# Weight tiles of a two-layer transformer kernel, moved to other byte positions in SBUF

## Chip, cores and metric

The kernel runs on one core of one Trainium2 chip. The metric is the device time of one execution in microseconds. Before the change the median of two runs is 2096.75 us (2096.28 to 2097.22).

## What is computed

Two transformer layers over 512 tokens (16 meta tokens are put ahead of the first) with a width of 1024, batch 1, all in float32. Cut to the projections, which are nearly all of the work:

```python
# first layer
p = rms_norm(h) @ w_in                       # pooling, attention, convolution, gates
y_a, y_b, y_c = pool(p) @ w_a, sparse_attention(p) @ w_b, conv(p) @ w_c
h = h + (g0 * y_a + g1 * y_b + g2 * y_c) @ w_o
h = h + (silu(gate) * up) @ w_down           # gate, up = rms_norm(h) @ w_gate_up, d_ff 2816
x = rms_norm(h)[16:]
# second layer
x = x + 0.5 * swiglu(rms_norm(x))            # d_ff 2816
x = x + merged(forgetting_attention, stick_breaking_attention) @ w_out
x = x + 0.5 * swiglu(rms_norm(x))            # d_ff 2816
x = x + sigmoid(rms_norm(x) @ w_ple_gate) * (p @ w_ple_proj)
```

## The kernel before

Activations lie transposed: feature on the partition, token on the free axis. hT (1024 x 528) is the residual. For a projection, each normed activation is split into a high and a low part, xh and xl, of 8 tiles with 128 x 576 columns, of which 528 are used (16 meta columns, then 512 tokens).

Weights come in 174 chunks. A chunk holds 2048 columns of 128 partitions: 8 contraction tiles of 256 output features. SyncE loads chunk c into raw[:, c % 2]. ScalarE copies it to whi as float32r (`high`, L1005; in the two attention stages of the second layer piece by piece, L1305), GpSimd subtracts to get wlo (`low`, L454, four instructions per chunk), and TensorE reads both. So raw, whi and wlo have two slots each, and a chunk's slot is c % 2. The next high tile of a slot is written when the chunk that used it is done.

TensorE makes three matmuls per contraction tile (`passes`, L543 to L547). The weights are the loaded operand and the activation is streamed:

```python
pe.matmul(o, w_of(whi), xhi, start=first, stop=False)    # L545
pe.matmul(o, w_of(whi), xlo, start=False, stop=False)    # L546
return pe.matmul(o, w_of(wlo), xhi, start=False, stop=last)   # L547
```

with `w_of = lambda wt: wt[:, s, w * k + o0:w * k + o0 + m]`. For a full chunk the piece of contraction tile k begins 1024 k bytes into the slot, plus 512 for the second half of the outputs; both are multiples of 256. The streamed piece is `hi[:, k, META:TM]`: 512 columns, 64 bytes into a row of 2304 bytes. Six chunks of the first layer (C_U to C_CB - 1) and the latent chunk C_LAT stream all 528 columns, in two parts of 264 (1056 bytes).

Where the streamed operand is not xh and xl it is: fh and fl in the three down projections (`ffn`, 528 matmuls each, three chunks of 8, 8 and 6 contraction tiles), ath, mh, m2h, ah, coh, yfh and ysh and their low parts in the mixer projections, pTh in the last. In `tokens` (L832 to L834, four chunks: the values of the two attentions of the second layer) xh and xl are loaded and whi and wlo are streamed, 256 columns at a time. C_FL is a chunk of 8 tiles with eight output features, 32 bytes each. `norm_sums` (L596 to L601), `head_sums` (L805) and the transposes (L759, L896, L903) are plain float32 matmuls with ones, onesblk or ident.

The order of the work is written out by hand, engine by engine; in the attention stages the single steps of the attention are set between the contraction tiles of chunks.

The tiles are allocated one behind the other in SBUF, in the order of the listing. By the built program, these are the first bytes in a partition, and that modulo 256:

```
tile        before          after
xh          18496  (64)     18496  (64)
xl          36928  (64)     36928  (64)
raw         55424  (128)    55424  (128)
whi slot 0  71808  (128)    71808  (128)
whi slot 1  80000  (128)    80128  (0)
wlo slot 0  88192  (128)    88512  (192)
wlo slot 1  96384  (128)    96832  (64)
rs          104576 (128)    105152 (192)
ident       113024 (128)    113600 (192)
arena, fh0  118144 (128)    118656 (128)
fh1         118272 (0)      118784 (0)
fh2         118336 (64)     118848 (64)
```

fh0 serves the first layer's FFN, fh1 and fh2 the two of the second layer; the low parts fl lie at the same place modulo 256. The operands of the mixer projections and pTh lie in the arena at 128 modulo 256.

Of the kernel before, what the change touches and what calls it, by code (L numbers as in the profile page):

```python
# [21 lines left out]
F32R = mybir.dt.float32r  # L22
# [4 lines left out]
P = 128  # L27
# [8 lines left out]
CH = 2048  # L36
# [67 lines left out]
def build(nc, I, out):  # L104
    with ExitStack() as ctx:
        def sb(name, shape, dt=F32):
            return ctx.enter_context(nc.sbuf_tensor(name, shape, dt))
# [9 lines left out]
        eps = sb("eps", [P, 1])  # L117
        m8 = sb("m8", [P, 8])
        raw = sb("raw", [P, 2, CH])
        whi = sb("whi", [P, 2, CH], F32R)  # L120
        wlo = sb("wlo", [P, 2, CH], F32R)
        rs = sb("rs", [P, TM])
        rt = sb("rt", [P, TM])
        sq = sb("sq", [P, TM])
# [16 lines left out]
        rtok = sb("rtok", [P, QB])  # L141
        fbias = sb("fbias", [8, 1])
        arena_cols = 27648
        pad = sb("pad", [P, (128 - (nc.sbuf_base + 31) // 32 * 32) % 256 // 4 or 64])
        start = (nc.sbuf_base + 31) // 32 * 32
        arena = sb("arena", [P, arena_cols])

# [1877 lines left out]
```

## Time and profile before

| | |
|---|---|
| runs, median | 2096.75 us |
| profiled execution, its own time | 2097.18 us |
| its span, first to last instruction | 2095.4 us |
| mean granted TensorE clock | 0.999 |
| TensorE matmul / weight load busy | 2053.9 / 1671.5 us |
| VectorE / ScalarE / GpSimd busy | 884.6 / 754.2 / 999.5 us |
| DMA | 184 MB, mean 88 GB/s |

The profiled execution is 0.4 us over the median. A matmul's recorded duration includes its way through the array and overlaps with the next matmul; its end is modelled. So the sum of durations is more than the time, and the pace of TensorE is the distance between two starts.

### The profile page before, as it was taken

The page shows a single profiled execution, that of the slowest core. Times are in us where ns is not written, and L with a number is a line of the kernel's source. Part 1 is how long each engine was busy: PE and PEld are TensorE (multiplying, and loading weights), DVE is VectorE, ACT ScalarE, POOL GpSimd, SP SyncE. Part 2 cuts the span into 40 slices and gives each one's busy share as a digit, 9 for nine tenths or more (in the row PEclk, how much of TensorE's full clock was granted, in tenths as well). Part 3 has the DMA queues.
Part 4 walks back from the last instruction along what each step waited for, and adds up shares of the span by engine and source line. Part 5 has one row for each costly group of instructions (what it writes and reads, how often), then busy time and mean ns, then how long its engine had stood idle before and what let it go on. Part 6 is the DMA issues. An engine that isn't in the chain of part 4 may idle for free.

```text
span 2095.4 us, 26593 instructions
## 1 busy us (share of the span) xinstructions
PE 2053.9 (98%) x9561; PEld 1671.5 (80%) x9561; DVE 884.6 (42%) x1394; ACT 754.2 (36%) x1038; POOL 999.5 (48%) x753
## 2 busy tenths in 40 slices
PE   8999999999999999999999999998899999999999
PEld 7798886688888888888888887886578888888877
DVE  6788735534333321343333124565653533331114
ACT  6412224434222223322222234666654332222232
POOL 5345442145555554455554445554434455554443
PEclk9999999999999999999999999999999999999999
DMA  4232331113333323333332232111113333332232
GB/s 156 71 96 81 101 100 61 41 60 100 101 100 100 92 88 107 95 96 88 97 100 91 95 96 81 61 50 52 41 61 101 100 99 88 94 100 95 91 105 81
DMA packets 250057, 184.01 MB, mean 88 GB/s; under 512 B 7040, under 2 KB 247168, under 8 KB 249984
## 3 DMA queue, kind: packets, MB, share of 16 engines
q1 hardware_dynamic: 249296, 182.74, 29.0%
q8 instruction: 44, 0.72, 0.1%
q10 hardware_dynamic: 688, 0.31, 0.1%
q14 instruction: 29, 0.24, 0.0%
HBM read 180.93 MB, written 2.10 MB: 87 GB/s over the span
## 4 chain that ended last, share of the span: by engine, by line
PE 89%; DVE 4%; ACT 2%; POOL 2%; issue 1%; DMA 0%; SPq 0%; DVEq 0%; ACTq 0%; POOLq 0%
PE ps L545 27%; PE ps L547 27%; PE ps L546 27%; POOL wlo L454 2%; DVE sc L1435 1%; PE ps L766 1%; PE ps L751 1%; PE ps L832 1%; PE ps L834 1%; PE ps L833 1%; DVE pu L1936 1%; PE ps L909 1%; DVE ssum L1563 0%; PE ps L765 0%; ACT whi L1305 0%
## 5 line engine op out<-in xcount | busy, mean ns | idle before, releaser
L454 POOL TENSOR_TENSOR wlo<-raw,whi 128x512 fp32r<-128x512 f32 (+1 forms) x692 | 938.2, 1386 | 978.3 <-ACT whi L1005 924.7
L545 PE MATMUL ps<-xh,whi 128*128 128x512 f32 (+2 forms) x1912 | 736.6, 385 | 12.9 <-DVE xl L1435 7.4
L547 PE MATMUL ps<-xh,wlo 128*128 128x512 f32 (+2 forms) x1912 | 723.2, 378 | 0.0
L546 PE MATMUL ps<-xl,whi 128*128 128x512 f32 (+2 forms) x1912 | 722.8, 378 | 0.0
L1005 ACT ACTIVATE whi<-raw 128x2048 fp32r<-128x2048 f32 (+1 forms) x159 | 297.5, 1871 | 802.3 <-PE ps L547 799.8
L545 PEld LDWEIGHTS ps<-xh,whi 128*128 128x128 f32 (+1 forms) x1912 | 359.4, 188 | 82.9 <-issue 11.7
L547 PEld LDWEIGHTS ps<-xh,wlo 128*128 128x128 f32 (+1 forms) x1912 | 358.6, 188 | 68.4
L546 PEld LDWEIGHTS ps<-xl,whi 128*128 128x128 f32 (+1 forms) x1912 | 359.4, 188 | 64.5 <-issue 2.5
L1489 DVE TENSOR_TENSOR tmp<-ps,rs 128x512 f32<-128x512 f32 x148 | 102.1, 692 | 325.8 <-PE ps L547 308.6
L545 PE MATMUL ps<-fh,whi 128*128 128x512 f32 x528 | 207.3, 393 | 0.0
L546 PE MATMUL ps<-fl,whi 128*128 128x512 f32 x528 | 207.3, 393 | 0.0
L547 PE MATMUL ps<-fh,wlo 128*128 128x512 f32 x528 | 207.3, 393 | 0.0
L1435 DVE SCALAR_TENSOR_TENSOR hT<-ps,hT 128x512 f32 x40 | 27.6, 691 | 279.0 <-PE ps L547 278.9
L1514 DVE TENSOR_TENSOR tmp<-tmp 128x512 f32<-128x512 f32 x66 | 90.2, 1367 | 114.3 <-ACT tmp L1047 114.2
L547 PEld LDWEIGHTS ps<-fh,wlo 128*128 128x128 f32 x528 | 99.0, 187 | 23.2
L546 PEld LDWEIGHTS ps<-fl,whi 128*128 128x128 f32 x528 | 99.0, 187 | 23.0
L545 PEld LDWEIGHTS ps<-fh,whi 128*128 128x128 f32 x528 | 99.0, 187 | 23.0
L1010 ACT ACTIVATE xh<-hT,vec (+1 forms) x48 | 34.5, 725 | 127.2 <-DVE hT L1435 127.2
L1049 ACT ACTIVATE fh<-tmp 128x512 f32 x66 | 41.8, 633 | 101.2 <-DVE tmp L1514 101.2
L1517 DVE TENSOR_TENSOR fl<-tmp,fh 128x512 f32 x66 | 51.1, 774 | 61.2 <-ACT fh L1049 61.2
L1435 DVE SCALAR_TENSOR_TENSOR xl<-hT,vec,xh (+1 forms) x48 | 46.0, 968 | 55.1 <-ACT xh L1010 54.9
L1047 ACT ACTIVATE tmp<-tmp 128x512 f32<-128x512 f32 x66 | 40.4, 612 | 2.9 <-DVE tmp L1489 2.9
(296 smaller groups left out, 2178.3 us busy)
## 6 DMA issues: line engine op xcount, KB each, us to landing
raw<-in_w_in SPq DMA_DIRECT2D x90, 512.0 KB, 4.6
raw<-in_w_gate_up SPq DMA_DIRECT2D x44, 512.0 KB, 4.7
raw<-in_ffn_w_gate SPq DMA_DIRECT2D x44, 512.0 KB, 4.0
raw<-in_ffn_w_up SPq DMA_DIRECT2D x44, 512.0 KB, 5.2
raw<-in_ffn_w_down SPq DMA_DIRECT2D x32, 512.0 KB, 4.3
raw<-in_w_down SPq DMA_DIRECT2D x16, 512.0 KB, 4.0
raw<-in_ffn_w_down SPq DMA_DIRECT2D x16, 384.0 KB, 3.4
raw<-in_w_b SPq DMA_DIRECT2D x8, 512.0 KB, 4.1
```

The lines of the kernel that those rows point to most:

```text
L454: ins = pool.tensor_tensor(wlo[:, c % 2, cs], raw[:, c % 2, cs], whi[:, c % 2, cs].bitcast(F32), ALU.subtract)
L545: pe.matmul(o, w_of(whi), xhi, start=first, stop=False)
L546: pe.matmul(o, w_of(whi), xlo, start=False, stop=False)
L547: return pe.matmul(o, w_of(wlo), xhi, start=False, stop=last)
L1005: act.activation(whi[:, c % 2, 0:n], raw[:, c % 2, 0:n], ACT.Copy).then_inc(w_hi, 1)
L1010: act.activation(one(xh, nn)[:, lo:TM], one(hT, nn)[:, lo:TM], ACT.Copy, scale=col(vec, lin(gain + n, per, i))).then_inc(xh_done, 1)
L1047: act.activation(tmp[:, 1, :], tmp[:, 0, :], ACT.Silu).then_inc(silu_done, 1)
L1049: act.activation(one(fh[f], lin(n, per, i)), tmp[:, 3, :], ACT.Copy).then_inc(h_hi, 1)
L1435: return dve.scalar_tensor_tensor(o, a, s, b, op0, op1)
L1489: dve.tensor_tensor(o, ps[0:o.shape[0], bank(c, t), :], rsx[0:o.shape[0]], ALU.mult).then_inc(acc_free, 1)
L1514: dve.tensor_tensor(tmp[:, 3, :], tmp[:, 1, :], tmp[:, 2, :], ALU.mult).then_inc(h_done, 1)
L1517: dve.tensor_tensor(one(fl[f], nn), tmp[:, 3, :], one(fh[f], nn).bitcast(F32), ALU.subtract).then_inc(h_split, 1)
```

## The change

High and low weight tiles get rows of 2080 columns, of which 2048 are used as before; between them stands a tile of 16 columns that nothing uses. So the four places (high or low, slot 0 or 1) differ modulo 256 bytes. The pad ahead of the arena is left out where its size would be zero, and the arena begins at 128 modulo 256 as before. The instructions of all five engines stand in the same order, with the same operands in the same sizes; only addresses differ. Of the tiles between wlo and the arena (rs, rt, sq, ssum, ident, identr, ones, causalr, strictr, onesblk and small ones) all move by 64 modulo 256.

```diff
-        whi = sb("whi", [P, 2, CH], F32R)
-        wlo = sb("wlo", [P, 2, CH], F32R)
+        whi = sb("whi", [P, 2, CH + 32], F32R)
+        aside = sb("aside", [P, 16])
+        wlo = sb("wlo", [P, 2, CH + 32], F32R)
...
-        pad = sb("pad", [P, (128 - (nc.sbuf_base + 31) // 32 * 32) % 256 // 4 or 64])
+        lead = (128 - (nc.sbuf_base + 31) // 32 * 32) % 256 // 4
+        if lead:
+            sb("pad", [P, lead])
```

## Rows read from the trace of the kernel before

**Rows 1.** The page: busy time, granted clock in 40 slices, the chain by engine and line.

```profile
PE 2053.9 (98%) x9561; PEld 1671.5 (80%) x9561; DVE 884.6 (42%) x1394; ACT 754.2 (36%) x1038; POOL 999.5 (48%) x753
...
PEclk9999999999999999999999999999999999999999
...
PE 89%; DVE 4%; ACT 2%; POOL 2%; issue 1%; DMA 0%; SPq 0%; DVEq 0%; ACTq 0%; POOLq 0%
PE ps L545 27%; PE ps L547 27%; PE ps L546 27%; POOL wlo L454 2%; DVE sc L1435 1%; PE ps L766 1%; PE ps L751 1%; PE ps L832 1%; PE ps L834 1%; PE ps L833 1%; DVE pu L1936 1%; PE ps L909 1%; DVE ssum L1563 0%; PE ps L765 0%; ACT whi L1305 0%
```

**Rows 2.** Waits of TensorE: waiting line, releaser: us in total, times, longest.

```profile
PE ps L545 <- DVE xl L1435: 7.4, 1, 7.4
PE ps L946 <- DVE pu L1937: 7.2, 10, 1.7
PE ps L545 <- POOL wlo L454: 5.0, 6, 1.2
```

**Rows 3.** Tile wlo, windows 755:873, 900:1100, 1116:1238, 1912:2034; durations min/median/max, starts.

```profile
L547 PE MATMUL ps<-fh,wlo x174: 387/389/396, 755.1 to 872.8; 128*128 128x512 f32 x174
...
L547 PE MATMUL ps<-xh,wlo x295: 389/389/389, 899.7 to 1099.6; 128*128 128x512 f32 x148
...
L547 PE MATMUL ps<-fh,wlo x175: 392/398/398, 1116.0 to 1237.8; 128*128 128x512 f32 x175
...
L547 PE MATMUL ps<-fh,wlo x175: 394/394/394, 1912.1 to 2033.9; 128*128 128x512 f32 x175
```

**Rows 4.** Tile wlo, window 104:135, two 264-column parts.

```profile
L547 PE MATMUL ps<-xh,wlo x86: 282/284/286, 103.9 to 134.9; 128*128 128x264 f32 x86
```

**Rows 5.** Timeline of TensorE in chunk C_FL; start, duration in us.

```profile
1289.71 0.40 PE L546 MATMUL ps<-xl,whi 128*8 128x512 f32 x1
...
1291.79 0.40 PE L546 MATMUL ps<-xl,whi 128*8 128x512 f32 x1
```

**Rows 6.** Timeline of TensorE in chunk C_FK + 1, after the head sums.

```profile
1276.37 0.40 PE L546 MATMUL ps<-xl,whi 128*128 128x512 f32 x1
...
1278.45 0.39 PE L546 MATMUL ps<-xl,whi 128*128 128x512 f32 x1
...
1279.59 0.39 PE L545 MATMUL ps<-xh,whi 128*128 128x512 f32 x1
...
1284.57 0.39 PE L546 MATMUL ps<-xl,whi 128*128 128x512 f32 x1
```

**Rows 7.** Groups by line and form: count, busy us, mean ns.

```profile
L545 PE MATMUL ps<-xh,whi 128*128 128x512 f32 x1680 | 667.6, 397 | 5.0 <-POOL wlo L454 5.0
...
L545 PE MATMUL ps<-fh,whi 128*128 128x512 f32 x528 | 207.3, 393 | 0.0
...
L545 PE MATMUL ps<-ath,whi 128*128 128x512 f32 x64 | 25.0, 391 | 1.2 <-DVE gb L1489 1.2
...
L759 PE MATMUL ps<-ident,pr 128*128 128x128 f32 x80 | 14.0, 274 | 0.6 <-issue 0.5
...
L545 PE MATMUL ps<-ah,whi 128*128 128x512 f32 x32 | 12.4, 389 | 0.0
```

**Rows 8.** Timeline of TensorE in the token chunk C_FV.

```profile
1298.92 0.28 PE L832 MATMUL ps<-whi,xh 128*128 128x256 f32 x1
...
1300.00 0.28 PE L832 MATMUL ps<-whi,xh 128*128 128x256 f32 x1
```

**Rows 9.** Busy us of each engine from 1300 to 1600 us.

```profile
1300.00:1600.00 300.00, 278.36 (x1479) 221.08 (x1478) 167.42 (x321) 179.68 (x369) 133.53 (x104) 0.99 0.19 60
```

**Rows 10.** Timelines of ScalarE and GpSimd around one chunk; start, us, idle before.

```profile
1006.89 1.92 ACT L1005 ACTIVATE whi<-raw 128x2048 fp32r<-128x2048 f32 x1 [6.29 <-PE ps L547]
...
1017.77 1.92 ACT L1005 ACTIVATE whi<-raw 128x2048 fp32r<-128x2048 f32 x1 [6.27 <-PE ps L547]
...
1008.89 5.95 POOL L454 TENSOR_TENSOR wlo<-raw,whi 128x512 fp32r<-128x512 f32 x4 [4.94 <-ACT whi L1005]
```

## Prediction

> **What bounds the kernel now.** I read the page first. TensorE's matmul row is busy 98% of the span, the chain that ended last lies on TensorE for 89%, and 81% stands on the three lines L545 to L547 [rows 1]; the granted clock is 0.9 or more of 2.4 GHz in all 40 slices, so this is the higher of its two levels throughout [rows 1]. All waits of matmuls that the trace names are short: the longest groups are 7.4, 7.2 and 5.0 us in total [rows 2]. So TensorE's own pace sets the end, and the question is whether the place of a weight tile in a 256-byte line is part of that pace.
>
> A busy share doesn't tell the pace, because matmuls overlap. What tells it is the distance from one start to the next. The view of the low tile gives, for a stretch, the first and last start of L547 and their count; between two of them lie three matmuls. At 2.4 GHz 512 columns take 512/2.4 = 213.3 ns. Measured: xh stream, 294 x 3 steps in 199.9 us = 226.6 ns; first FFN's down projection, 173 x 3 steps in 117.7 us = 226.8; second FFN's down, 174 x 3 in 121.8 us = 233.3; third FFN's down, the same 233.3 [rows 3].
>
> The four streams run one loop with the same counts and weights. What differs is where the streamed operand begins in a line of 256 bytes. By the layout, whi and wlo begin at byte 128, both slots. xh and xl begin at 64, and META skips 64 more: 128. The first FFN's fh at 128, the second's at 0, the third's at 64. So where streamed operand and weights begin at the same place the step is 226.7 ns, and where they don't it is 233.3. In the second FFN the steps aren't alike: the modelled durations lie between 392 and 398 ns, where they are 389 at a step of 226.7 and 394 at 233.3 [rows 3]. On that scale 398 is a step of some 238 ns, and the short one, since two of them take 2 x 233.3, some 229. In the third FFN all steps are alike (394 throughout).
>
> Two groups warn that this isn't all. With 264 columns, streamed from bytes 64 and 96 against weights at 128, the step is 31.0/(85 x 3) = 121.6 ns, against 110.0 for the columns alone: an excess of 11.6, less than the 13.3 of the equal places [rows 4]. And the eight-column weights of C_FL, 32 bytes each, give 2.08 us for 9 steps = 231.1 with the streamed operand at 128 [rows 5], so the place of the streamed operand alone doesn't secure 226.7. After other operations cut in, a chunk begins with 2.08 us for 9 steps, 231.1 each, and a little later goes 4.98 us for 22 steps, 226.4 [rows 6]. So some state of the two reads is carried on from one matmul to the next.
>
> **The change, part by part.** The instruction order of every engine is the same. Only addresses move.
>
> *The high and low tiles.* In line bytes: high, slot 0 at 128 and slot 1 at 0; low, slot 0 at 192 and slot 1 at 64. Streamed operands stay. Full-width matmuls with the streamed operand at 128 are 3 x 1680 = 5040 (xh), 528 of the 1584 on fh, 3 x (3 x 64 + 4 x 32) = 960 in the mixer projections (ath, mh and m2h with 64 per line, ah, coh, yfh and ysh with 32) and 48 in the last one: 6576 [rows 7]. In slot 0 the two high passes stay equal and the low one doesn't; in slot 1 none is equal. Chunks alternate between slots, so (1/3 + 1)/2 = 2/3 lose the equal place: 4384. At 233.3 - 226.7 = 6.6 ns that is +28.9 us. High slot 1 against 128 is a distance of 128 bytes, that of the second FFN; low slot 0 a distance of 64 bytes, that of the third. Low slot 1 lies 64 bytes behind, which no long stream here shows; I take 6.6 too.
>
> *The other two FFNs.* In the second (streamed from 0) the high passes of slot 1 become equal, 528 x 2/3 x 1/2 = 176, and in the third (from 64) the low passes of slot 1, 88: 264 x 6.6 = -1.7 us.
>
> *Token and 264-column matmuls.* The 384 token matmuls swap the roles (xh is loaded, the weights are streamed) and step at 1.08/9 = 0.12 us [rows 8]; 2/3 of them lose the equal place. The nearest rows are the 264-column ones, where unequal places cost nothing: I take 0, with -0.4 to +1.7 us as ends (256 x -1.7 or +6.6 ns). The 672 of 264 columns (six chunks of 96 and the latent one) are unequal before and nearly all after: 0.
>
> *Cover.* From 1300 to 1600 us the matmul row is busy 278 of 300 us, so there PE waits for others [rows 9], and slower matmuls use up part of these waits. The 12 full chunks from C_SQ to the last gate, 48 matmuls each, and part of the 4 beside the first attention lie in such stretches, some 700 matmuls: 700 x 2/3 x 6.6 ns = 3 us; I take half as hidden: -1.5 us.
>
> *The other tiles.* `aside` is never read. rs to fbias shift by 64 bytes modulo 256. Of the matmuls on them the transposes with ident are the most, 80 on L759 [rows 7] and as many on L896 and on L903: at 6.6 ns each for 240 that would be 1.6 us, and since operand and identity differ in form from the passes I take 0. VectorE, ScalarE and GpSimd read and write at new places. A chunk's high tile starts at 1006.89, the low one ends at 1008.89 + 5.95 = 1014.84, and PE is done with its chunk at 1017.77, when the next conversion starts [rows 10]. That is 2.9 us of slack, so GpSimd's 5.95 us could grow by half before PE waited; without this cover each added microsecond would count once per chunk, 174 times. 0.
>
> Sum: 28.9 - 1.7 - 1.5 = +25.7 us. Against the profiled execution's own 2097.2 that gives 2122.9, and against the median of the runs, 0.4 lower, 2122.5.
>
> *Bounds of a changed matmul.* From above: the long step of the second FFN, 238, is +11.3 ns: +50 us on 4384, and +74 if all 6576 take it. From below: the excess of the 264-column rows, 11.6 instead of 13.3, is -1.7 ns or -7 us; further down nothing goes under the columns themselves, -13.3 ns or -88 us on 6576, and no row of full width comes near that. I take 6.6, as 1044 steps of full width show it.
>
> **Rivals.**
>
> *The place of the weights doesn't matter, only that of the streamed operand.* Then 128 is a good beginning and 0 and 64 are bad ones, whatever the weights do; time 2096.7. For it: in this trace all full chunks' weights begin at 128, so [rows 3] can't separate the two. Against it: the C_FL row, slow at 128. A page of the Trainium skill goes this way: "TensorE: Matmul & The Clock Gate", Part 2, step 1, says that TensorE reads its streamed operand and its weights over two independent ports, so that loading weights takes nothing from the running matmul. By that rule the sum is 0. The trace shows no such freedom in sum, since two streams that differ in nothing but place step at 226.8 and 233.3 [rows 3]; it leaves open which of the two reads is slowed.
>
> *The stream no longer settles at all.* High and low passes now alternate between places, and [rows 6] show that a disturbance lasts some ten matmuls. Then all 6576 go at 233.3: 6576 x 6.6 = +43.4, less 1.5: 2139. Where the alternating step of the second FFN rules, up to 2169. For it: [rows 6]. Against it: in the second and third FFN every matmul is unequal, and a mean over 233.3 appears in neither.
>
> *The other side: spread places part the two reads, and it gets faster.* If weights and streamed operand at one place contend for one part of a line, a distance takes that away, as with 264 columns. Mechanism: the excess falls from 13.3 to 11.6 on 4384 matmuls, -7 us: 2089; it decides from where a distance of 64 or 128 bytes costs less than none. Against it: the second and third FFN have just these distances and are slower. Only the low tile's slot 1, a sixth of the matmuls, has a distance not seen.
>
> **How the numbers follow.** Forecast (own range 2112 to 2132): 0.47. Streamed operand alone: 0.25. Nothing settles, 2133 or more: 0.20. Faster: 0.08. Predicted time 2122.5. For 8 in 10 the range takes in the no-change case and the first part of the unsettled one, 2090 to 2148; left out are most of the faster case and the upper part of the unsettled one. The borders of 2%, about what a measurement of this kernel can tell from no change, are at 2054.8 and 2138.7. Slower by more: half of the unsettled case and a little of the forecast's tail, 0.14. Faster by more would need an excess cut by 6.4 ns on 6576 matmuls: 0.02. Within: 0.84.
>
> **What would show it.** Right: in the xh stream between 900 and 1100 us chunks alternate between about 228.9 ns a step (slot 0) and 233.3 (slot 1), mean 231.1; the first FFN's down goes from 226.8 to about 231, the second's and third's from 233.3 to some 231 and 232. The waits stay as short, and GpSimd and ScalarE keep their times. Wrong: the same 226.7 in the xh stream (only the streamed place counts), or any step under it, or second and third FFN unmoved while the rest grows.

## Result and profile after

The changed kernel takes 2124.69 us (median of two runs, 2123.73 to 2125.66) against 2096.75: ratio 1.0133, 95% interval 1.0114 to 1.0152, 27.9 us slower. The forecast was 2122.5. The profiled execution has a span of 2123.8 us, 28.4 over that of [rows 1].

First the page of the changed kernel: busy times of the engines, the granted clock, the chain by engine. Lines L545 to L547 are now L548 to L550.

```profile
PE 2082.2 (98%) x9561; PEld 1673.7 (79%) x9561; DVE 886.5 (42%) x1394; ACT 754.3 (36%) x1038; POOL 1005.0 (47%) x753
...
PEclk9999999999999999999999999999999999999999
...
PE 90%; DVE 4%; POOL 2%; ACT 2%; issue 2%; DMA 0%; SPq 0%; DVEq 0%; ACTq 0%; POOLq 0%
```

Against [rows 1], TensorE's matmul row is 28.3 us longer, as much as the span; the weight loads grew by 2.2 us, and no other engine by more than 5.5. The count of instructions is the same, and the mean granted clock is 0.998 for 0.999. So TensorE takes longer for the same work, and doesn't wait more: the longest groups of waits are those of [rows 2], within 1.5 us.

```profile
PE ps L548 <- DVE xl L1438: 7.4, 1, 7.4
PE ps L949 <- DVE pu L1940: 6.8, 9, 1.6
PE ps L548 <- POOL wlo L457: 6.5, 5, 2.0
```

On the clock the 40 slices, some 52 us each, hide something. In the kernel before, the clock falls to the lower level, 1.2 GHz, for a few microseconds from 1515.1 us. TensorE had just stood idle for 1.66 us in the second layer's attention. The view of a stretch within it gives the stretch, its length, TensorE's busy time, the granted clock as a share of 2.4 GHz, and the DMA's share and GB/s:

```profile
1515.20:1518.40 3.20, 3.20 (x9) 0.50 0.00 0
```

The changed kernel has two such falls, from 24.0 and from 1454.2 us. So the clock wasn't at the higher level throughout, as the prediction read it from [rows 1]. None of these falls lies in a stretch from which a step is read below.

The view of the tile wlo, in the stretches that answer to [rows 3] (durations min/median/max in ns, then first and last start in us):

```profile
L550 PE MATMUL ps<-fh,wlo x176: 389/397/400, 768.2 to 889.9; 128*128 128x512 f32 x176
...
L550 PE MATMUL ps<-xh,wlo x292: 389/397/398, 914.0 to 1116.4; 128*128 128x512 f32 x146
...
L550 PE MATMUL ps<-fh,wlo x176: 387/397/400, 1137.3 to 1259.1; 128*128 128x512 f32 x176
...
L550 PE MATMUL ps<-fh,wlo x176: 387/392/398, 1940.8 to 2061.8; 128*128 128x512 f32 x176
```

| stream | before | forecast | after |
|---|---|---|---|
| xh, 900 to 1100 us | 226.6 ns a step | 231.1 | 202.4 us / (291 x 3) = 231.8 |
| first FFN's down | 226.8 | 231 | 121.7 / (175 x 3) = 231.8 |
| second FFN's down | 233.3 | 231 | 121.8 / 525 = 232.0 |
| third FFN's down | 233.3 | 232 | 121.0 / 525 = 230.5 |

Within the xh stream the two slots of the chunks differ. The timeline of TensorE, a chunk of slot 0 and then one of slot 1 (start, duration in us):

```profile
1004.63 0.39 PE L548 MATMUL ps<-xh,whi 128*128 128x512 f32 x1
...
1012.49 0.39 PE L549 MATMUL ps<-xl,whi 128*128 128x512 f32 x1
1012.72 0.40 PE L550 MATMUL ps<-xh,wlo 128*128 128x512 f32 x1
1012.95 0.39 PE L548 MATMUL ps<-xh,whi 128*128 128x512 f32 x1
...
1016.42 0.40 PE L548 MATMUL ps<-xh,whi 128*128 128x512 f32 x1
...
1022.72 0.40 PE L548 MATMUL ps<-xh,whi 128*128 128x512 f32 x1
```

Slot 0: 36 steps in 8.32 us, 231.1 ns. Slot 1: 27 steps in 6.30 us, 233.3. Over whole chunks of this stream, with the change of slot, it is 230.9 and 233.0. The forecast had 228.9 and 233.3, so slot 1 came out as told, and slot 0 loses twice what was expected.

GpSimd's low tile is as far from the path as in [rows 10]: it starts when the high one is done and takes the same 5.95 us.

```profile
1016.52 5.95 POOL L457 TENSOR_TENSOR wlo<-raw,whi 128x512 fp32r<-128x512 f32 x4 [5.09 <-ACT whi L1008]
```

Two parts of the kernel keep their time. The 264-column matmuls answer to [rows 4]:

```profile
L550 PE MATMUL ps<-xh,wlo x78: 282/285/287, 111.8 to 139.9; 128*128 128x264 f32 x78
```

28.1 us / (77 x 3) = 121.6 ns, as before. And the two attention stages of the second layer, where full chunks stand between the steps of the attention, take as long as they did; each of the two traces has one fall of the clock in them. Here are the first kt matmul and the first yfh matmul, of the kernel before (views of the tiles kt and yfh):

```profile
L866 PE MATMUL ps<-kt,qt x32: 220/332/429, 1319.1 to 1412.2; 128*128 128x128 f32 x8, 128*128 128x256 f32 x8, 128*128 128x384 f32 x8, 128*128 128x512 f32 x8
...
L545 PE MATMUL ps<-yfh,whi x32: 387/389/398, 1584.2 to 1624.4; 128*128 128x512 f32 x32
```

and of the kernel after:

```profile
L869 PE MATMUL ps<-kt,qt x32: 220/335/423, 1340.4 to 1433.8; 128*128 128x128 f32 x8, 128*128 128x256 f32 x8, 128*128 128x384 f32 x8, 128*128 128x512 f32 x8
...
L548 PE MATMUL ps<-yfh,whi x32: 387/390/404, 1605.5 to 1646.6; 128*128 128x512 f32 x32
```

1584.2 - 1319.1 = 265.1 us before, 1605.5 - 1340.4 = 265.1 after, with twelve full chunks in it. What the fall at 1515 us costs the kernel before shows beside two kernels of the experiments that have none in these stages: the same stretch takes 263.4 us in fh_all_128, whose weights and xh stand as before, and 263.9 in w192, where every full-width matmul in it has a distance of 64.

### The profile page after: what moved, and what is told of

The parts are those of the page before. It is cut to its first block, busy times and chain, and to the rows that moved or that the text cites. A ratio compares the mean times of both kernels' runs of the same rounds, so it can differ in the third digit from the quotient of the medians.

```text
span 2123.8 us, 26593 instructions
## 1 busy us (share of the span) xinstructions
PE 2082.2 (98%) x9561; PEld 1673.7 (79%) x9561; DVE 886.5 (42%) x1394; ACT 754.3 (36%) x1038; POOL 1005.0 (47%) x753
## 4 chain that ended last, share of the span: by engine, by line
PE 90%; DVE 4%; POOL 2%; ACT 2%; issue 2%; DMA 0%; SPq 0%; DVEq 0%; ACTq 0%; POOLq 0%
PE ps L548 28%; PE ps L550 28%; PE ps L549 27%; POOL wlo L457 2%; DVE sc L1438 1%; PE ps L769 1%; PE ps L912 1%; PE ps L835 1%; PE ps L754 1%; PE ps L836 1%; PE ps L837 1%; DVE pu L1939 0%; PE ps L768 0%; PE ps L762 0%; PE ps L808 0%
## 5 line engine op out<-in xcount | busy, mean ns | idle before, releaser
L548 PE MATMUL ps<-xh,whi 128*128 128x512 f32 (+2 forms) x1912 | 742.7, 388 | 14.5 <-DVE xl L1438 7.4
L550 PE MATMUL ps<-xh,wlo 128*128 128x512 f32 (+2 forms) x1912 | 733.1, 383 | 0.0
L548 PEld LDWEIGHTS ps<-xh,whi 128*128 128x128 f32 (+1 forms) x1912 | 359.0, 188 | 89.6 <-issue 11.7
L550 PEld LDWEIGHTS ps<-xh,wlo 128*128 128x128 f32 (+1 forms) x1912 | 358.1, 187 | 75.1
L550 PE MATMUL ps<-fh,wlo 128*128 128x512 f32 x528 | 208.2, 394 | 0.0
L548 PE MATMUL ps<-fh,whi 128*128 128x512 f32 x528 | 208.2, 394 | 0.0
L550 PEld LDWEIGHTS ps<-fh,wlo 128*128 128x128 f32 x528 | 99.1, 188 | 23.4
L548 PEld LDWEIGHTS ps<-fh,whi 128*128 128x128 f32 x528 | 99.2, 188 | 22.2
```

## Experiments

In all of them a distance is the place of the loaded weights minus that of the streamed operand, modulo 256 bytes. Every kernel without a note on rounds was timed once, beside the kernel before at 2096.45 to 2096.78 us; what is read from them rests on the steps in the traces, which one profile shows to a tenth of a nanosecond in the mean over some hundred matmuls.

### All weights at one other place: w192, w0, w64

```diff
+        ahead = sb("ahead", [P, 16])     # w192; 32 for w0, 48 for w64
         whi = sb("whi", [P, 2, CH], F32R)
         wlo = sb("wlo", [P, 2, CH], F32R)
+        behind = sb("behind", [P, 48])   # w192; 32 for w0, 16 for w64
```

> Before, with both slots of whi and wlo at byte 192 of a 256-byte line instead of 128; all other tiles keep their places modulo 256. Theory R (the distance between the place of the loaded weights and that of the streamed operand decides): the distance in the xh stream, the first FFN's down and the mixer projections is 64, as in the third FFN before, so 233.3 ns a step there, evenly; second FFN (distance 192) and third (128) about 233.3; time 2096.7 + 6576 x 6.6 ns - 1.5 = 2139 us. Rival M (mixing: high and low tiles or slots at different places disturb each other, a single place costs nothing): 226.7 ns in the xh stream, time 2097. Rival A (byte 128 is the good place for weights, whatever is streamed): 233.3 or more in all streams.

> Before, with both slots of whi and wlo at byte 0. R: xh stream at distance 128, as the second FFN before: 233.3 ns in the mean with unlike steps (durations 392 to 398); the second FFN's down, streamed from 0, falls to 226.7; time 2096.7 + 43.4 - 3.5 - 1.5 = 2135 us. A: the second FFN's down doesn't fall to 226.7. M: 226.7 in the xh stream, time 2097 or less.

> Before, with both slots of whi and wlo at byte 64. The xh stream gets the distance of the low tile's slot 1 in the changed kernel (192, or 64 behind), which no trace has shown alone. R: about 233.3 ns there, and 226.7 in the third FFN's down, streamed from 64; time about 2135 us. If this distance is worse than the others (240 ns), it explains the part by which the changed kernel's slot 1 would be slow: time 2175. A: the third FFN's down stays at 233.3 or over.

Measured: w192 2129.74 us, w0 2125.66, w64 2110.87. The xh stream of w192 in the view of the tile wlo:

```profile
L549 PE MATMUL ps<-xh,wlo x286: 393/396/398, 905.1 to 1104.6; 128*128 128x512 f32 x143
```

199.5 us / (285 x 3) = 233.3 ns. The same view of w0 shows the xh stream and the second FFN, whose operand is streamed from byte 0:

```profile
L549 PE MATMUL ps<-xh,wlo x286: 392/395/398, 904.8 to 1104.3; 128*128 128x512 f32 x143
...
L549 PE MATMUL ps<-fh,wlo x162: 389/389/389, 1140.0 to 1249.5; 128*128 128x512 f32 x162
```

233.3 ns in xh, and 109.5/(161 x 3) = 226.7 in the second FFN. In w64 it is the third FFN, streamed from 64, that falls; the first rows are its first FFN and its xh stream, both at distance 192:

```profile
L549 PE MATMUL ps<-fh,wlo x173: 392/392/392, 761.4 to 879.5; 128*128 128x512 f32 x173
...
L549 PE MATMUL ps<-xh,wlo x286: 397/397/398, 904.8 to 1104.3; 128*128 128x512 f32 x143
...
L549 PE MATMUL ps<-fh,wlo x162: 389/389/389, 1935.0 to 2044.5; 128*128 128x512 f32 x162
```

118.1/(172 x 3) = 228.9, then 233.3, then 109.5/483 = 226.7. Rival A (128 is the good place for weights) falls with the two 226.7, and rival M (a single place costs nothing) with the 233.3. That the place of the weights doesn't matter falls too, since here it alone was moved. R stands. Two things R hadn't said: distance 192 runs at 228.9 in some stretches and at 233.3 in others of the same kernel, so a stream has more than one pattern that it can hold; and the totals of all three lie 9 to 24 us under the expected 2139, 2135 and 2135. For w192 most of it has its places: the 16 chunks beside the three attentions hardly pay, 768 matmuls x 6.6 ns = 5 us of which 1.5 had been counted; its second FFN, at distance 192, fell to 228.9, 2.3 us, and its third, at 128, to 232.4, 0.5 us; the token matmuls got 1 us shorter (see the last section); and it has no fall of the clock in the attention stages, which costs the kernel before 1.7 us. For w0 it is the third FFN, at distance 192 and 228.9 (2.3 us), the first layer behind its attention, at 232.4 to 232.5 (some 2 us), and the same 16 chunks. For w64 it is the cheaper pattern, which all its settled streams at distance 192 took but the gate projections of the second FFN.

The falls of the clock give one thing more. Here is the one of the kernel before, with weights and stream at one place, and that of w0, at distance 128:

```profile
1515.84 0.63 PE L546 MATMUL ps<-xl,whi 128*128 128x512 f32 x1
...
1517.97 0.63 PE L545 MATMUL ps<-xh,whi 128*128 128x512 f32 x1
```
```profile
1453.36 0.63 PE L548 MATMUL ps<-xl,whi 128*128 128x512 f32 x1
...
1455.49 0.51 PE L547 MATMUL ps<-xh,whi 128*128 128x512 f32 x1
```

Five steps take 2.13 us in both, 426 to 427 ns each, and in the falls of w64, hi128_lo192 and the changed kernel the starts stand 426 to 427 ns apart as well. That is 512 columns at 1.2 GHz, 426.7 ns, with nothing on top. So at the lower clock the place costs nothing, and the 13.3 ns over the columns at equal places are gone too; both appear only at 2.4 GHz.

### Everything moved together: all_by_64

```diff
+        ahead = sb("ahead", [P, 16])
         hT = sb("hT", [P, DK, TM])
...
-        pad = sb("pad", [P, (128 - (nc.sbuf_base + 31) // 32 * 32) % 256 // 4 or 64])
+        pad = sb("pad", [P, (192 - (nc.sbuf_base + 31) // 32 * 32) % 256 // 4 or 64])
```

> Before, with every tile moved on by 64 bytes together: weights and arena at 192, streamed xh at 192. R: nothing changes, 226.7 ns in the xh stream and the first FFN, 233.3 in the second and third, time 2096.7 (within 0.2%). A, or any theory with places counted from a fixed line start: xh stream at 233.3, time about 2139.

Measured: 2096.75 us beside 2096.66. The xh stream holds 199.9 us for 294 x 3 steps, 226.6 ns, with every tile at another place:

```profile
L548 PE MATMUL ps<-xh,wlo x295: 389/389/389, 904.7 to 1104.6; 128*128 128x512 f32 x148
```

So places count against each other, not against a fixed line start. That they count modulo 256 bytes follows from the xh stream itself: from one contraction tile to the next the weights move on by 1024 bytes and the streamed row by 2304, so their difference changes by 1280, and the halves of the outputs add 512; the steps stay at 226 to 227 ns through all of them. What repeats must therefore divide 256, and 128 doesn't do, since distance 128 costs.

### Parts of the change: hi128_lo192, hi128_lo64, slots_128_0, others_by_64

```diff
         whi = sb("whi", [P, 2, CH], F32R)
+        between = sb("between", [P, 16])   # hi128_lo192; 48 for hi128_lo64
         wlo = sb("wlo", [P, 2, CH], F32R)
+        behind = sb("behind", [P, 48])     # hi128_lo192; 16 for hi128_lo64
```

> Before, with both slots of the high tile at 128 as they were and both of the low tile at 192: only the low pass has a distance (64) in the xh stream. Theory P (each pass pays for its own distance, as the forecast's sum had it): two passes at 226.7, one at 233.3, mean 228.9 in both slots, time 2096.7 + 6576 x 2.2 ns - 1 = 2110 us. Rival N (an unequal pass pulls its equal neighbours along): both slots like the changed kernel's slot 0, 230.9 in the mean, time 2096.7 + 6576 x 4.2 - 1 = 2123 us.

> Before, with the high tile at 128 and the low one at 64, so the low pass of the xh stream has the distance 192, the cheapest of the unequal ones (228.9 alone). P (each pass pays for itself): (2 x 226.7 + 228.9)/3 = 227.4, time 2096.7 + 6576 x 0.7 = 2101.5 us. N (the stream as a whole takes on one pattern): 231 as with the low tile at 192, time about 2120. In between: the disturbance follows the price of the distance, 228.9 in the mean, 2110.

Measured: 2119.55 and 2120.34 us. The xh stream of hi128_lo192, first by the tile view, then by the timeline:

```profile
L549 PE MATMUL ps<-xh,wlo x289: 397/397/398, 905.3 to 1105.0; 128*128 128x512 f32 x145
```
```profile
1004.19 0.39 PE L548 MATMUL ps<-xl,whi 128*128 128x512 f32 x1
1004.42 0.40 PE L549 MATMUL ps<-xh,wlo 128*128 128x512 f32 x1
1004.66 0.39 PE L547 MATMUL ps<-xh,whi 128*128 128x512 f32 x1
1004.89 0.39 PE L548 MATMUL ps<-xl,whi 128*128 128x512 f32 x1
```

199.7/(288 x 3) = 231.1 ns in the mean: P wanted 228.9. By the starts of the whole stretch, the step that begins with the low pass takes 235.8 ns, those of the two high passes 228.3 and 229.2; the high passes, which have no distance at all, don't get back to 226.7. How the loss lies on the three can't be put down to each pass's own distance, for the loads run ahead. They start 2 to 3 ns behind the start of the matmul before:

```profile
1004.20 0.19 PEld L549 LDWEIGHTS ps<-xh,wlo 128*128 128x128 f32 x1
1004.42 0.19 PEld L547 LDWEIGHTS ps<-xh,whi 128*128 128x128 f32 x1
```

So the low weights, the ones with a distance, are loaded while the pass of xl streams, in a step of 229.2 ns, and in the longest step the load is one with no distance. With the low tile at distance 192, the cheapest one alone, the mean is the same:

```profile
L549 PE MATMUL ps<-xh,wlo x289: 389/398/403, 905.2 to 1104.9; 128*128 128x512 f32 x145
```

N holds in both: a stream in which one pass in three is out of place takes a pattern of its own, and what that costs, 4.4 ns a matmul over 226.7, doesn't follow the price of the one distance.

```diff
-        whi = sb("whi", [P, 2, CH], F32R)
-        wlo = sb("wlo", [P, 2, CH], F32R)
+        whi = sb("whi", [P, 2, CH + 32], F32R)
+        wlo = sb("wlo", [P, 2, CH + 32], F32R)
```

> Before, with slot 0 of both tiles at 128 and slot 1 of both at 0: within a chunk all passes have one distance. P and N agree if a stream settles within a chunk: chunks of slot 0 at 226.7 and of slot 1 at 233.3 in the xh stream; time 2096.7 + 3288 x 6.6 - (264 x 6.6, second FFN) - (264 x 4.4, third) - 1 = 2114.5 us. If the stream keeps its state over the chunk border, slot 0 stays over 230 and the time comes to about 2125.

Measured: 2110.19 us. The shortest duration in its xh stream is the 389 of 226.7, the longest 405:

```profile
L547 PE MATMUL ps<-xh,wlo x291: 389/390/405, 904.9 to 1104.7; 128*128 128x512 f32 x146
```

199.8/(290 x 3) = 229.7 in the mean, where 230.0 was expected. With one place per chunk the pattern ends at the chunk's border: chunks of slot 0 are back at the step of equal places, and only the others pay. The timeline, 27 steps in a chunk of slot 1, then 27 in one of slot 0:

```profile
985.64 0.39 PE L545 MATMUL ps<-xh,whi 128*128 128x512 f32 x1
...
991.92 0.40 PE L545 MATMUL ps<-xh,whi 128*128 128x512 f32 x1
...
996.06 0.39 PE L545 MATMUL ps<-xh,whi 128*128 128x512 f32 x1
...
1002.18 0.39 PE L545 MATMUL ps<-xh,whi 128*128 128x512 f32 x1
```

6.28 us are 232.6 ns a step, 6.12 us are 226.7.

```diff
         wlo = sb("wlo", [P, 2, CH], F32R)
+        behind = sb("behind", [P, 16])
```

> Before, with whi and wlo where they were and the tiles behind them (rs, rt, sq, ssum, ident, identr, ones, causalr, strictr, onesblk and small ones) moved by 64 bytes, as the change moves them. Theory: this part of the change costs nothing, 2096.7 us (within 0.1%). Rival: fp32 matmuls, scans and GpSimd work at new places cost, up to the 1.6 us of the 240 transposes or more, and account for a share of the 28 us.

Measured: 2096.53 us beside 2096.45. The moved vectors, constants and sums cost nothing that can be seen (0.1 us), so all of the 28 us is the weight tiles'.

### Finer places: fh_160_224_32, fh_96_192_128

```diff
-F_AT = (0, 32, 48)
+F_AT = (8, 24, 40)      # fh_160_224_32; (56, 16, 0) for fh_96_192_128
```

> Before, weights at 128, with the FFN activations at 160, 224 and 32 instead of 128, 0 and 64: distances (weights minus streamed) of 224, 160 and 96. Tells how fine the grain is. If places count in pieces of 64 bytes (a 32-byte shift stays in the piece or half crosses): first FFN's down near 226.7 or between that and 228.9, second near 228.9 to 233.3, third 233.3. If any distance costs alike: 233.3 in all three, time 2096.7 + 528 x 6.6 = 2100. If a distance is cheaper than none: under 226.7 somewhere, and a better kernel follows.

> Before, with the FFN activations at 96, 192 and 128: distances 32, 192 and 0. First FFN's down 233.3 (32 bytes were as bad as 64 in the other direction), second 228.9 or 233.3 (both were seen at distance 192), third 226.7. Time 2096.7 + 3.5 - (0 to 2.3) - 3.5, so 2094.5 to 2096.7. If distance 32 is cheap, the first is under 230 and the time lower by 2 us.

Measured: 2100.39 us and 2095.89. The down projections of fh_160_224_32, at distances 224, 160 and 96:

```profile
L547 PE MATMUL ps<-fh,wlo x158: 393/395/397, 759.9 to 869.8; 128*128 128x512 f32 x158
...
L547 PE MATMUL ps<-fh,wlo x158: 399/399/399, 1124.9 to 1234.8; 128*128 128x512 f32 x158
...
L547 PE MATMUL ps<-fh,wlo x157: 392/397/400, 1919.8 to 2029.5; 128*128 128x512 f32 x157
```

and the first two of fh_96_192_128, at 32 and 192 (its third, at distance 0, is at 226.7):

```profile
L547 PE MATMUL ps<-fh,wlo x158: 395/396/396, 759.7 to 869.6; 128*128 128x512 f32 x158
...
L547 PE MATMUL ps<-fh,wlo x161: 392/392/392, 1124.7 to 1234.5; 128*128 128x512 f32 x161
```

All distances that were run, with 512 streamed float32r columns and high and low alike (two numbers where stretches of one distance differ; the 232.5 is the first FFN's down of w0, and w192's third stands at 232.4):

| distance in bytes | 0 | 32 | 64 | 96 | 128 | 160 | 192 | 224 |
|---|---|---|---|---|---|---|---|---|
| ns a step | 226.7 | 233.3 | 233.3 | 234.4 | 233.3, 232.5 | 233.3 | 228.9, 233.3 | 233.3 |

So 32 bytes are as bad as 128; there is no grain of 64. And nothing is cheaper than distance zero.

### The better kernel: fh_all_128

```diff
-F_AT = (0, 32, 48)
+F_AT = (0, 0, 0)
```

> Before, with the FFN activations of all three FFNs at byte 128, where the weights are. Theory R (distance zero is the cheapest of all places): second and third FFN's down go from 233.3 to 226.7 ns a step, 2 x 522 x 6.6 ns = 6.9 us less: 2089.8 us, a ratio of 0.9967, faster than both kernels. If the streamed place 128 were not enough: 2096.7.

Measured over five rounds: 2088.96 us (2088.43 to 2090.48) beside 2096.78, ratio 0.9965, 95% interval 0.9952 to 0.9979. The second and third FFN's down projections in its tile view:

```profile
L547 PE MATMUL ps<-fh,wlo x176: 389/389/390, 1115.9 to 1234.9; 128*128 128x512 f32 x176
...
L547 PE MATMUL ps<-fh,wlo x176: 389/389/390, 1906.9 to 2025.9; 128*128 128x512 f32 x176
```

119.0/525 = 226.7 both, in place of 233.3: 7 us, and the kernel is 7.8 faster. The rest lies in the clock. Three of the five runs, and three of the nine of the kernel before beside them, have a mean granted clock of 1.000; among these the medians are 2088.57 and 2095.57 us, 7.0 apart. It beats both kernels. This is the opposite of the change: all operands of a matmul at one place, instead of four.

## Why the prediction was right, point by point

- *Where the time goes.* Shown: TensorE's own pace, +28.3 us of matmul row with the same count and the same waits. The clock wasn't at its higher level throughout, as the prediction has it, but that moved little: the one run of the changed kernel with a mean granted clock of 1.000 takes 2123.73 us, and the kernel before at 1.000 takes 2095.57 (the median of three runs), 28.2 less.
- *The distance decides, not the streamed place alone* (the rival with 0.25). Shown by w192, w0 and w64, which move the weights alone, and by all_by_64, which moves all. The Trainium skill, "TensorE: Matmul & The Clock Gate", Part 2, step 1, says that loading the next tile's weights takes no SBUF read bandwidth from the running matmul. In sum this trace doesn't bear that out: with the loads at other places the same stream goes from 226.7 to 233.3. Which of the two reads is held up, and by what, no run shows. The recorded weight loads keep their 187 to 188 ns, and a matmul without a weight load beside it wasn't tried.
- *Slot 1.* High passes at distance 128 and low ones at 192, 6.6 ns each: 233.3 forecast, 233.3 measured. The 6.6 for distance 192, taken without a row, is one of the two values that w64 shows alone (228.9 in most of its streams). Since single prices don't add up in a stream of unlike passes, as slot 0 shows, this hit is partly luck.
- *Slot 0, the term that was mis-sized.* The sum let each pass pay for its own distance: two at 226.7 and one at 233.3. Measured 231.1, since the unequal pass changes the pattern of all three; hi128_lo192 shows this with both slots alike. A slot 0 matmul loses 4.4 ns, not 2.2. The rival in which the stream no longer settles had this mechanism, but with too much: it let all matmuls go to 233.3, and named [rows 6] as its evidence, which hold here only in that a stream carries a state.
- *The second and third FFN* were to gain 1.7 us together; they gained 522 x 1.3 and 522 x 2.8 ns, 2.1 us. The second gained less than told (232.0 for 231), the third more (230.5 for 232).
- *Cover.* Forecast 1.5 us from half of some 700 matmuls. Measured: the 12 chunks of the second layer's attention stages lose nothing, 265.1 us before and after. With the 4 of the first layer, which lose 0.3 us together, that is 768 matmuls, of 5.2 ns each: 4.0 us, nearly all of it saved. The traces show two reasons. Take fh_all_128 and w192, which have no fall of the clock there. Where a full-width pass follows another directly and without a wait in these stages (468 steps under 245 ns in each), the mean step is 229.7 and 233.2 ns: streams that are broken off again and again lose 3.5 ns and not 6.6. That makes 1.6 us, yet the stages are only 0.5 us longer (263.9 for 263.4), so the waits cover most of the rest.
- *Tokens and 264 columns*: 0 forecast; 121.6 ns before and after for 264 columns, and 119.8 to 119.1 ns for the token matmuls, 0.3 us less.
- *Other tiles*: 0 forecast, 0.1 us measured by others_by_64.

With the measured sizes: 5808 settled full-width matmuls from 226.7 to 231.9 give 30.2, the two FFNs -2.1, the rest 0: 28.1 of the 28.4 us of the span. The forecast's 25.7 is close partly by luck, because misses cancel: slot 0 costs 6576/2 x 2.2 = 7.2 us more; against it the 768 matmuls beside the attentions take 2.8 away beyond the 1.5 forecast, the two slots at 230.9 and 233.0 over whole chunks 1.6, and the FFNs 0.4.

## What to carry to other kernels

Where float32r matmuls of 512 columns stand back to back at the higher clock, put the tile that is loaded and the tile that is streamed at the same place modulo 256 bytes, for every operand that meets these weights; here that is worth 6.6 of 233.3 ns a matmul, and the existing kernel gains 0.35% from it with one line. Don't spread double-buffered slots or high and low parts over a line. For matmuls of 256 columns, measure anew: the token matmuls go the other way. Judge such a change by the distance from start to start over some hundred matmuls: the busy share was 98% in every kernel here.

## What was not expected

- A matmul's step isn't a function of its own operands. With one pass in three out of place the steps of the two others are longer as well (231.1 in the mean, for 228.9 by sum), and distance 192 ran at 228.9 ns in one stretch and 233.3 in another of the same kernel.
- Most streams take one of four means: 226.7, 228.9, 231.1 and 233.3 ns, 13.3, 15.6, 17.8 and 20.0 over the columns' own 213.3, evenly 2.2 ns apart. 232.4 to 232.5 (most of w0's first layer, the third FFN of w192) and 234.4 (distance 96) don't fit. That 512 columns alone take 213.3 is half of the 426.7 measured at half the clock.
- A shift by 32 bytes costs as much as one by 128 (233.3 both).
- With 264 columns (121.6 ns before and after) none of this shows, and in the time of the attention stages hardly any.
- At the lower clock the step is 426.7 ns at every distance that a fall of the clock met (0, 128 and 192, and 64 in one pass of three): the places cost something only at 2.4 GHz.
- The token matmuls stream 256 columns of weights against a loaded xh. Equal places are the dearest for them: 119.8 ns a step in the kernel before, 117.3 in w192 and 117.0 in w64. What the forecast's third rival said of 512 columns, that a distance shortens the step, holds here; why, no run shows. The low pass of two of the four chunks, in the kernel before and then in w192:

```profile
L833 PE MATMUL ps<-wlo,xh x63: 281/283/283, 1296.5 to 1318.8; 128*128 128x256 f32 x63
```
```profile
L835 PE MATMUL ps<-wlo,xh x63: 280/280/280, 1320.4 to 1342.3; 128*128 128x256 f32 x63
```
